# Three places reordered: a second gate bank in the up-projections, the first merge gate scaled inside the attention, a square root ahead of an exponential

## The chip, the core and the metric

The kernel runs on one core of one Trainium2 chip. The metric is the device time in microseconds (us) of one execution of the whole program, taken as the median of several. The engines are TensorE (PE, whose weight loads are shown as PEld), VectorE (DVE), ScalarE (ACT), GpSimd (POOL) and SyncE (SP, which issues the transfers). They run side by side and meet only at semaphores.

## The reference, cut to what matters

Two transformer stacks run one behind the other over 512 tokens of width 1024, all in float32. The first stack has two layers, the second has two. The parts that the change touches:

```python
# first stack, feed forward: causal convolution of width 3 on the gate, exact gelu
u, g = split(h @ w_in, 2)                 # 2816 columns each
g = causal_conv3(g) * w + b
out = (gelu(g) * u) @ w_out
# second stack, per layer
q, k = rope(rmsnorm(q)), rope(rmsnorm(k)) # axial attention: 8 query heads, 2 key heads
p = softmax(q @ k.T); ya = p @ v
z = [y_n @ w_branch[n] for n in range(3)] # ya axial, yb pooling, yc neighbourhood
merged = sum(sigmoid(gl_n + b_n) * z_n for n in range(3))
```

## The kernel before, in words

**Layout.** Activations lie transposed, features in partitions and the 512 tokens in the free dimension, so one tile is 128x512. Every projection is done to about float32 accuracy by splitting both operands in a head and a remainder: one product of 128x128 weights with a 128x512 tile is three matmuls (L476, L477, L478: head by head, head by remainder, remainder by head). A projection over 1024 features is eight such products, 24 matmuls, into one PSUM bank. The eight banks are called PA, PB, S0, S1, T0, T1, O0 and O1. POOL makes the heads and remainders of the weights (L456, L458), in two slots that PE empties in turn; SP refills the raw weights behind it.

**Order of the work.** Each engine has its own program, written out by hand, and the engines wait on counters: `pa_taken` and `pb_taken` say how often the content of PA and PB has been read out, `entry_done` how many weight entries PE has finished, `p_ready` how many exponentials, `pt_copied` how many transposed tiles ACT has copied out. Each engine works strictly in the order of its own program.

**Up-projections (L875 on PE, L1768 on DVE, L1272 on ACT).** There are 22 units, each a gate tile (into PA) and a value tile (into PB). Before unit 0 can be scaled, the norm's factor is needed: PE sums the squares in the middle of the first value tile (L503), ACT takes the root (L1122) and DVE the reciprocal (L1399). DVE then takes the gate (L1777), does the convolution (L1758, L1761, L1761), takes the value (L1782), multiplies it with ACT's gelu (L1788) and writes the remainder (L1790). PE may begin the next gate when PA has been taken, and the next value when PB has. `up` with `squared` false is the first stack's (it runs twice, up0 and up1), with `squared` true the second stack's.

**Axial attention (L662 on PE, L1192 on ACT, L1577 on DVE).** 32 steps t, one per head and query tile, four groups of eight. At an even t PE issues the scores of t and t+1 (L699). DVE scales them and takes their minimum (L1483), ACT takes the exponential (L1169, `soften`), PE transposes it two steps later (L610), ACT copies the transpose out (L1175, `copy_turned`), and PE multiplies by the values three steps later, two heads at once (L742). In between PE fills in parts of the next query projection, three products at t % 8 = 0 and 1, two at 2 in the first three groups; from t = 24 on the slots hold none, one or two products of the next stage. A query group is also normalized on the way: at t % 8 = 5 PE sums squares per head (L815), at t % 8 = 6 ACT takes the root of these sums from bank PB (L1258, `q_root`), at t % 8 = 7 DVE inverts it (L1615). At t = 15, 23, 27 and 35 PE spreads the denominators of a finished group over a bank (L759, `den_turn`): for the first three that bank is PB, and for t = 15 and t = 23 it waits until `q_root` of step 14 or 22 has read PB. ACT copies the spread denominators (L1237), DVE divides (L1525, `y_divide`, at t + 2), ACT and DVE write head and remainder (L1241, L1529, at t + 3 and t + 4). ACT has to load another table when it goes from exponential to root and back (rows named ACT_TABLE_LOAD).

**Merge (L935 on PE, L1280 on ACT, L1793 on DVE).** 24 gates, three per output tile. For each, PE projects the gate into PA (24 matmuls) and the branch into PB (12 matmuls), DVE scales the gate by the norm's factor (L1800), ACT takes the sigmoid (L1287), DVE multiplies it with the branch (L1804 for the first of three, L1806 and L1808 for the others). The first gate and the first branch are projected inside the last twelve steps of the neighbourhood attention, t = 24 to 35; the gate is complete at t = 31. Its scaling by L1800 comes after the whole attention on DVE, so after `y_divide` and the last remainder, and the second gate waits for it since it goes to PA too.

Of the kernel before, what the change touches and what calls it, by code (L numbers as in the profile page):

```python
# [8 lines left out]
ALU = mybir.AluOpType  # L9
# [5 lines left out]
FT = 22  # L15
# [167 lines left out]
def build(nc, x_in, weights, consts, cols_in, lam_in, rel_in, rpb_in, strips_rel, strips_na, out):  # L183
    with ExitStack() as ctx:
# [284 lines left out]
        def _(pe):  # L469
# [192 lines left out]
            def attention(b, b0, kind, last_parts=(), last_plan=()):  # L662
# [18 lines left out]
                def span(t):  # L681
                    return S if full else (t // 2 % 4 + 1) * P
# [20 lines left out]
                for t in range(end + 1):  # L703
                    if t < 32 and t % 2 == 0:
                        score(t); score(t + 1)
                    if t in turns:
                        (y_turn if kind == "diff" else den_turn)(b, turns.index(t), kind)
# [11 lines left out]
                    if 0 <= tt < 32:  # L719
                        if tt < 2:  # L720
                            pe.wait_ge(v_copied, 4 * b["v"] - 1 + tt)
                        pe.wait_ge(p_ready, u + tt + 3)
                        pe.wait_ge(pt_copied, u + tt + 1)
                        transposed(tt, span(tt)).then_inc(pt_ready, 1)
                    tv = t - 3
                    if 0 <= tv < 32:
# [148 lines left out]
            def up(b, squared):  # L875
# [19 lines left out]
                else:  # L895
# [3 lines left out]
                    project(PB[:, :], 1, b["e"] + 1, sum_of=b).then_inc(entry_done, 1)  # L899
                with pe.Fori(1, FT) as i:  # L900
                    gate_and_value(i)
# [149 lines left out]
            H = here  # L1051
# [51 lines left out]
        def _(act):  # L1103
# [88 lines left out]
            def attention(b, kind, ytile, early=None, gain=None):  # L1192
# [4 lines left out]
                for t in range(turns[3] + (2 if kind == "diff" else 4)):  # L1197
                    if t == 4 and early is not None:
                        early()
                    if t < 32:  # L1200
                        soften(u, t, S if full else (t // 2 % 4 + 1) * P,
                               (diff_ready, 4 * b["df"] + max(t // 2 - 1, 0)) if kind == "diff" else None,
                               maps[t // 2 % 2] if kind == "diff" else probs)
# [9 lines left out]
                    if kind == "axial" and t < 24:  # L1213
                        bn = axial_turn(b, t // 8 + 1)
                        if t % 8 == TURN["square"]:
                            q_square(bn["a"] + 2, gain)
                        if t % 8 == TURN["root"]:
                            q_root(bn["r"])
                    if kind == "diff" and t % 2 == 0 and 0 <= t - 8 < 32:
# [154 lines left out]
        def _(dve):  # L1374
# [201 lines left out]

            def attention(b, kind, ytile, after=None):  # L1577

# [9 lines left out]
                for t in range(turns[3] + (3 if kind == "diff" else 5)):  # L1588
# [29 lines left out]
                    if kind != "axial" and t < 24 and t % 8 == K_AT:  # L1618
                        take_k(ahead(g), g + 1)
                    if after is not None and t == 29:  # L1620
                        take_q(after, 0)
# [146 lines left out]
            def up(b, col, two):  # L1768
                per = 5 if two else 2
                taps = [(1, 0), (0, 1), (2, -1)] if two else [(2, 0), (1, 1), (0, 2)]  # L1770
                sum_factor(b)
                with dve.Fori(0, FT) as i:
                    sum_waited(b)
                    chain_at(b["d"] + 1 + i * per)
                    dve.wait_ge(entry_done, b["e"] + 2 * i + 3)
                    dve.wait_ge(gelu_ready, b["z"] + i + 1)
                    TT(GATE[:, :], PA[:, :], rs[:, :], ALU.mult).then_inc(pa_taken, 1)  # L1777
                    dve.wait_ge(pa_taken, b["a"] + i + 2)
# [12 lines left out]
                    done(per)  # L1791

            def merge(b):  # L1793
                with dve.Fori(0, 4) as i:
                    chain_at(b["d"] + i * 2)
                    for q in range(6):
                        n, j = q % 3, 2 * i + q // 3
                        dve.wait_ge(gate_ready, 24 * b["l"] + 6 * i + q + 1)
                        dve.wait_ge(gate_done, 24 * b["l"] + 6 * i + q + 1)
                        TT(tmp[3][:, :], PA[:, :], rs[:, :], ALU.mult).then_inc(pa_taken, 1)  # L1800
                        dve.wait_ge(entry_done, b["e"] + 6 * i + q + 3)
                        dve.wait_ge(gate_done, 24 * b["l"] + 6 * i + q + 2)
                        if n == 0:
                            TT(tmp[1][:, :], PB[:, :], tmp[0][:, :], ALU.mult).then_inc(pb_taken, 1)  # L1804
                        else:
                            TT(tmp[2][:, :], PB[:, :], tmp[0][:, :], ALU.mult).then_inc(pb_taken, 1)  # L1806
                            dve.wait_ge(pb_taken, b["b"] + 6 * i + q + 2)
                            ins = TT(tmp[1][:, :], tmp[1][:, :], tmp[2][:, :], ALU.add)  # L1808
                            if n == 1:
                                link(ins)  # L1810
                            else:
                                ins.then_inc(m_f, 1)

                        if n == 2:
                            dve.wait_ge(m_hi, b["m"] + j + 1)
                            TT(tile(ml, j), tmp[1][:, :], tile(mh, j).bitcast(F), ALU.subtract).then_inc(m_split, 1)
                            dve.wait_ge(m_split, b["m"] + j + 1)
                    done(2)

            def pooling(b, kv, ax, l):  # L1820
# [85 lines left out]
            with dve.Fori(0, LAYERS2) as l:  # L1906
# [3 lines left out]
                v_copy(H("na_v", l))  # L1910
                attention(H("na", l), "na", 8)
                merge(H("merge", l))
# [190 lines left out]
```

## Time and profile before

| what | us |
|---|---|
| median of three runs | 3124.68 (3124.17 to 3125.82) |
| the profiled execution's own time | 3117.95 |
| its span, first to last instruction | 3115.7 |
| PE busy | 3016.9, 97% |
| POOL / DVE / ACT busy | 1659.7 / 1358.7 / 797.9 |
| mean granted TensorE clock | 0.992 of full |

The span is what the hardware profiler saw of the program; the own time is some 2 us more. "Busy" of PE is the time in which a matmul was under way, at whatever clock. The median of the runs is 6.7 us above the profiled execution, 0.2%.

### The profile page before, as it was taken

The page shows a single profiled execution, that of the slowest core. Times are in us where ns is not written, and L with a number is a line of the kernel's source. Part 1 is how long each engine was busy: PE and PEld are TensorE (multiplying, and loading weights), DVE is VectorE, ACT ScalarE, POOL GpSimd, SP SyncE. Part 2 cuts the span into 40 slices and gives each one's busy share as a digit, 9 for nine tenths or more (in the row PEclk, how much of TensorE's full clock was granted, in tenths as well). Part 3 has the DMA queues.
Part 4 walks back from the last instruction along what each step waited for, and adds up shares of the span by engine and source line. Part 5 has one row for each costly group of instructions (what it writes and reads, how often), then busy time and mean ns, then how long its engine had stood idle before and what let it go on. Part 6 is the DMA issues. An engine that isn't in the chain of part 4 may idle for free.

```text
span 3115.7 us, 44683 instructions
## 1 busy us (share of the span) xinstructions
PE 3016.9 (97%) x14804; PEld 2383.8 (77%) x14804; DVE 1358.7 (44%) x2339; ACT 797.9 (26%) x1459; POOL 1659.7 (53%) x1254
## 2 busy tenths in 40 slices
PE   8998999999899999999999999999999999999998
PEld 6766888886578888776678878888767688778886
DVE  3254444223444442243433476640543343576622
ACT  2343221113422220153421122210263411122201
POOL 4334666663156666433346656666324266556674
PEclk9999999999999999999999999999999999999999
DMA  6262223222022233212322222333113222222332
GB/s 160 77 174 73 94 95 107 103 95 74 26 70 92 97 106 107 86 41 67 90 72 91 88 74 97 98 105 104 64 38 90 64 92 97 85 74 96 100 111 78
DMA packets 99746, 276.63 MB, mean 89 GB/s; under 512 B 38014, under 2 KB 38782, under 8 KB 99634
## 3 DMA queue, kind: packets, MB, share of 16 engines
q1 hardware_dynamic: 97184, 269.03, 26.9%
q10 hardware_dynamic: 2450, 6.13, 0.9%
q8 instruction: 67, 1.10, 0.1%
q14 instruction: 45, 0.37, 0.0%
HBM read 271.39 MB, written 11.54 MB: 91 GB/s over the span
## 4 chain that ended last, share of the span: by engine, by line
PE 72%; DVE 2%; issue 1%; ACT 1%; DVEq 0%; ACTq 0%
PE PA L476 11%; PE PA L477 10%; PE PA L478 10%; PE PB L476 9%; PE PB L478 9%; PE PB L477 9%; PE O L742 2%; PE S L699 2%; PE T L610 2%; PE O L508 1%; DVE hl L1409 1%; PE PB L759 0%; DVE tmps L1448 0%; PE O L633 0%; PE S L586 0%
## 5 line engine op out<-in xcount | busy, mean ns | idle before, releaser
L458 POOL TENSOR_TENSOR wl<-raw,wh 128x1024 fp32r<-128x1024 f32 (+2 forms) x416 | 1127.0, 2709 | 33.4
L455 POOL TENSOR_TENSOR zero<-zero 128x1 f32<-128x1 f32 x416 | 82.6, 198 | 1391.4 <-PE PA L478 624.5
L476 PE MATMUL PA<-hh,wh 128*128 128x512 f32 x1328 | 537.1, 404 | 19.4 <-DVE hl L1409 7.1
L477 PE MATMUL PA<-hl,wh 128*128 128x512 f32 x1328 | 521.3, 393 | 0.0
L478 PE MATMUL PA<-hh,wl 128*128 128x512 f32 x1328 | 521.0, 392 | 0.0
L456 POOL CAST wh<-raw 128x1024 fp32r<-128x1024 f32 (+2 forms) x416 | 476.3, 1145 | 0.0
L476 PE MATMUL PB<-hh,wh 128*128 128x512 f32 x896 | 357.8, 399 | 0.0
L478 PE MATMUL PB<-hh,wl 128*128 128x512 f32 x896 | 349.3, 390 | 0.0
L477 PE MATMUL PB<-hl,wh 128*128 128x512 f32 x896 | 349.2, 390 | 0.0
L476 PEld LDWEIGHTS PA<-hh,wh 128*128 128x128 f32 x1328 | 251.9, 190 | 120.1 <-issue 55.5
L478 PEld LDWEIGHTS PA<-hh,wl 128*128 128x128 f32 x1328 | 251.5, 189 | 54.0
L477 PEld LDWEIGHTS PA<-hl,wh 128*128 128x128 f32 x1328 | 252.0, 190 | 51.2 <-issue 2.5
L1169 ACT ACTIVATE probs<-biased,stats 128x512 f32<-128x512 f32 (+2 forms) x224 | 145.2, 648 | 322.7 <-PE T L610 192.4
L1761 DVE SCALAR_TENSOR_TENSOR tmps<-S,cols,tmps 128x511 f32<-128x511 f32 (+1 forms) x264 | 197.9, 750 | 39.6 <-DVE tmps L1761 20.0
L476 PEld LDWEIGHTS PB<-hh,wh 128*128 128x128 f32 x896 | 168.1, 188 | 46.9 <-issue 14.6
L478 PEld LDWEIGHTS PB<-hh,wl 128*128 128x128 f32 x896 | 168.4, 188 | 36.0
L477 PEld LDWEIGHTS PB<-hl,wh 128*128 128x128 f32 x896 | 168.4, 188 | 33.9 <-issue 1.2
L1276 ACT ACTIVATE T<-tmps 128x512 f32<-128x512 f32 x88 | 53.0, 602 | 395.2 <-DVE tmps L1761 395.2
L1278 ACT ACTIVATE acth<-T 128x512 f32 x88 | 52.7, 599 | 333.2 <-DVE T L1788 333.2
L476 PE MATMUL PA<-acth,wh 128*128 128x512 f32 x352 | 137.4, 390 | 0.0
L478 PE MATMUL PA<-acth,wl 128*128 128x512 f32 x352 | 137.0, 389 | 0.0
L477 PE MATMUL PA<-actl,wh 128*128 128x512 f32 x352 | 137.0, 389 | 0.0
(321 smaller groups left out, 4828.3 us busy)
## 6 DMA issues: line engine op xcount, KB each, us to landing
raw<-in_w_up SPq DMA_DIRECT2D x176, 512.0 KB, 3.4
raw<-in_w_down SPq DMA_DIRECT2D x64, 768.0 KB, 4.1
raw<-in_w_merge SPq DMA_DIRECT2D x48, 768.0 KB, 4.2
raw<-in_w_out SPq DMA_DIRECT2D x32, 512.0 KB, 3.4
strips_na<-in_rpb SPq DMA_DIRECT2D x1, 7620.0 KB, 31.5
raw<-in_w_pool SPq DMA_DIRECT2D x12, 512.0 KB, 3.4
raw<-in_w_na_qk SPq DMA_DIRECT2D x12, 512.0 KB, 3.5
raw<-in_w_na_v SPq DMA_DIRECT2D x8, 512.0 KB, 3.4
```

Of the source, the lines that this page charges most:

```text
L455: nc.gpsimd.tensor_tensor(zero[:, :], zero[:, :], zero[:, :], ALU.add)
L456: nc.gpsimd.tensor_copy(wh[s][:, 0:width], raw[s][:, 0:width]).then_inc(w_head, 1)
L458: nc.gpsimd.tensor_tensor(wl[s][:, 0:width], raw[s][:, 0:width], wh[s][:, 0:width].bitcast(F), ALU.subtract).then_inc(w_split, 1)
L476: mm(dst, h_, rh, start=first, stop=False)
L477: mm(dst, h_, rl, start=False, stop=False)
L478: return mm(dst, l_, rh, start=False, stop=last)
L610: last = nc.tensor.transpose(TB[t % 2][:, k * P:k * P + P], src[t % 2][:, k * P:k * P + P], ident[:, :])
L699: mm(SB[head][:, 0:span(t)], queries[g % 2][r, qt * P:qt * P + P], (axial_key if kind == "axial" else keys[g % 2])[r, 0:span(t)], start=Tr ...
L742: last = mm(bank[r, q], values(head, k), probsT[head][:, k * P:k * P + P], start=(k == 0), stop=(k == L // P - 1))
L1169: A(to[t % 2][:, 0:L], biased[t % 2][:, 0:L], ACT.Exp, scale=-1.0, bias=mn[:, t % 8:t % 8 + 1], accum_out=den[:, t % 8:t % 8 + 1]).then_in ...
L1276: A(GELU[:, :], tmp[0][:, :], f).then_inc(gelu_ready, 1)
L1761: ins = STT(out=dst[:, lo:hi], in0=src[:, lo - d:hi - d], scalar=w(k), in1=dst[:, lo:hi], op0=ALU.mult, op1=ALU.add)
```

## The change

Three edits. **(1)** In `up` of the first stack, PE projects the second gate into O0 with no wait on `pa_taken`, and the second value into PB after its own wait; the loop starts at unit 2. DVE does units 0 and 1 ahead of its loop, the second reading its gate from O0. **(2)** DVE scales the merge's first gate at t = 35 of the neighbourhood attention, ahead of `y_divide` of t = 37; the merge's first round on DVE is written out without that step. A wait on `m_split` moves from behind the remainder (L1816) to the next first product of a group. **(3)** In the axial attention ACT does `q_root` at the head of step t, ahead of that step's exponential and copy, and PE does `den_turn` of t = 15 and t = 23 behind the transposition of that step.

```diff
 (PE, attention)
-                    if t in turns:
+                    late = kind == "axial" and t in turns[0:2]
+                    if t in turns and not late:
                         (y_turn if kind == "diff" else den_turn)(b, turns.index(t), kind)
...
                         transposed(tt, span(tt)).then_inc(pt_ready, 1)
+                    if late:
+                        den_turn(b, turns.index(t), kind)
...
 (PE, up)
                     project(PB[:, :], 1, b["e"] + 1, sum_of=b).then_inc(entry_done, 1)
-                with pe.Fori(1, FT) as i:
+                    project(O0[:, :], 0, b["e"] + 2).then_inc(entry_done, 1)
+                    pe.wait_ge(pb_taken, b["b"] + 2)
+                    project(PB[:, :], 1, b["e"] + 3).then_inc(entry_done, 1)
+                with pe.Fori(1 if squared else 2, FT) as i:
                     gate_and_value(i)
...
 (ACT, attention)
+                    if kind == "axial" and t < 24 and t % 8 == TURN["root"]:
+                        q_root(axial_turn(b, t // 8 + 1)["r"])
                     if t < 32:
                         soften(u, t, S if full else (t // 2 % 4 + 1) * P,
...
-                        if t % 8 == TURN["root"]:
-                            q_root(bn["r"])
...
 (DVE, attention)
+                    if gate is not None and t == 35:
+                        take_gate(gate, 0)
...
 (DVE, up)
-                with dve.Fori(0, FT) as i:
+                def unit(i, gate_bank):
...
-                    TT(GATE[:, :], PA[:, :], rs[:, :], ALU.mult).then_inc(pa_taken, 1)
+                    TT(GATE[:, :], gate_bank[:, :], rs[:, :], ALU.mult).then_inc(pa_taken, 1)
...
+                sum_factor(b)
+                if not two:
+                    unit(0, PA)
+                    unit(1, O0)
+                with dve.Fori(0 if two else 2, FT) as i:
+                    unit(i, PA)
...
 (DVE, merge)
+            def take_gate(b, n):
+                dve.wait_ge(gate_ready, 24 * b["l"] + n + 1)
+                dve.wait_ge(gate_done, 24 * b["l"] + n + 1)
+                TT(tmp[3][:, :], PA[:, :], rs[:, :], ALU.mult).then_inc(pa_taken, 1)
...
+                        if q >= taken:
+                            take_gate(b, 6 * i + q)
...
                         if n == 0:
+                            if taken == 0 or q:
+                                dve.wait_ge(m_split, b["m"] + j)
                             TT(tmp[1][:, :], PB[:, :], tmp[0][:, :], ALU.mult).then_inc(pb_taken, 1)
...
-                            dve.wait_ge(m_split, b["m"] + j + 1)
...
+                tiles(0, 1)
+                with dve.Fori(1, 4) as i:
+                    tiles(i, 0)
...
-                attention(H("na", l), "na", 8)
+                attention(H("na", l), "na", 8, gate=H("merge", l))
```

## Rows read from the trace of the kernel before

**Rows 1.** The page, busy us, share of the span and instructions.

```profile
PE 3016.9 (97%) x14804; PEld 2383.8 (77%) x14804; DVE 1358.7 (44%) x2339; ACT 797.9 (26%) x1459; POOL 1659.7 (53%) x1254
```

**Rows 2.** PE's waits: line, waited for, us in total, times, longest us.

```profile
PE PB L759 <- ACT stats L1258: 9.3, 4, 2.3
...
PE PA L476 <- DVE S L1777: 6.2, 2, 3.1
...
PE PA L476 <- DVE tmps L1800: 5.9, 2, 3.0
```

**Rows 3.** PE by stretch: us, busy (matmuls), granted clock, DMA share, GB/s.

```profile
300.00:304.00 4.00, 0.92 (x5) 1.00 0.23 89
...
1419.00:1421.00 2.00, 2.00 (x5) 0.50 0.00 0
1575.00:1578.00 3.00, 2.90 (x7) 0.56 0.00 0
2299.00:2301.00 2.00, 1.87 (x16) 0.50 0.00 0
```

**Rows 4.** Timeline, start of up0: start, us, engine, line [idle before, releaser].

```profile
300.43 0.40 PE L478 MATMUL PB<-hh,wl 128*128 128x512 f32 x1
...
303.90 0.49 PE L476 MATMUL PA<-hh,wh 128*128 128x512 f32 x1 [3.08 <-DVE S L1777]
...
306.78 0.69 DVE L1782 TENSOR_TENSOR tmps<-PB,rs 128x512 f32<-128x512 f32 x1
...
309.86 0.69 DVE L1777 TENSOR_TENSOR S<-PA,rs 128x512 f32<-128x512 f32 x1
...
314.90 0.39 PE L476 MATMUL PA<-hh,wh 128*128 128x512 f32 x1
```

**Rows 5.** Timeline, axial attention of layer 0, steps 13 to 16.

```profile
1388.51 0.58 ACT L1175 ACTIVATE probsT<-T 128x512 f32<-128x512 f32 x1
...
1389.27 1.09 PE L742 MATMUL O<-probsT,tmps 128*64 128x128 f32 x16
...
1391.07 1.28 ACT L1258 ACT_TABLE_LOAD   x1
...
1392.36 0.27 ACT L1258 ACTIVATE stats<-PB,eps 128x8 f32<-128x8 f32 x1
...
1392.68 1.09 PE L759 MATMUL PB<-ident,stats 128*64 128x128 f32 x16 [2.32 <-ACT stats L1258]
...
1395.74 0.72 ACT L1169 ACTIVATE probs<-biased,stats 128x512 f32<-128x512 f32 x1
...
1398.06 1.09 PE L742 MATMUL O<-probsT,tmps 128*64 128x128 f32 x16
```

**Rows 6.** Timeline, the same layer, steps 22 to 24.

```profile
1412.80 0.58 ACT L1175 ACTIVATE probsT<-T 128x512 f32<-128x512 f32 x1
...
1416.97 1.09 PE L759 MATMUL PB<-ident,stats 128*64 128x128 f32 x16 [2.32 <-ACT stats L1258]
...
1423.23 0.99 PE L742 MATMUL O<-probsT,tmps 128*64 128x128 f32 x14
```

**Rows 7.** Timeline, from the neighbourhood attention into the merge, layer 0.

```profile
1565.64 0.17 DVE L1519 RECIPROCAL stats<-stats 128x2 f32<-128x2 f32 x1 [0.28 <-ACT probs L1169]
...
1571.75 0.40 PE L478 MATMUL PB<-yh,wl 128*128 128x512 f32 x1
...
1572.87 0.63 ACT L1241 ACTIVATE yh<-y_tok 128x512 fp32r<-128x512 f32 x1 [0.91 <-DVE y_tok L1525]
1573.90 3.78 POOL L458 TENSOR_TENSOR wl<-raw,wh 128x1536 fp32r<-128x1536 f32 x1
1575.10 0.58 PE L476 MATMUL PA<-hh,wh 128*128 128x512 f32 x1 [2.95 <-DVE tmps L1800]
1577.33 0.69 DVE L1804 TENSOR_TENSOR tmps<-PB,tmps 128x512 f32<-128x512 f32 x1 [2.37 <-ACT tmps L1287]
...
1584.97 0.39 PE L476 MATMUL PA<-hh,wh 128*128 128x512 f32 x1
```

More of the change, by code:

```diff
@@ L1575, in take_k, with attention @@
                 TT(keys[g % 2][:, :], PB[:, :], rs[:, :], ALU.mult).then_inc(pb_taken, 1)
-            def attention(b, kind, ytile, after=None):
+            def attention(b, kind, ytile, after=None, gate=None):
                 u, turns = b["u"], Y_TURN[kind]
@@ L1770, in up @@
                 taps = [(1, 0), (0, 1), (2, -1)] if two else [(2, 0), (1, 1), (0, 2)]
-                sum_factor(b)
-                with dve.Fori(0, FT) as i:
+                def unit(i, gate_bank):
                     sum_waited(b)
@@ L1791, in up, with tiles @@
                     done(per)
+                sum_factor(b)
[8 more added lines that the diff above has]
+                TT(tmp[3][:, :], PA[:, :], rs[:, :], ALU.mult).then_inc(pa_taken, 1)
             def merge(b):
-                with dve.Fori(0, 4) as i:
+                def tiles(i, taken):
                     chain_at(b["d"] + i * 2)
@@ L1797, in merge @@
                         n, j = q % 3, 2 * i + q // 3
-                        dve.wait_ge(gate_ready, 24 * b["l"] + 6 * i + q + 1)
-                        dve.wait_ge(gate_done, 24 * b["l"] + 6 * i + q + 1)
-                        TT(tmp[3][:, :], PA[:, :], rs[:, :], ALU.mult).then_inc(pa_taken, 1)
+                        if q >= taken:
+                            take_gate(b, 6 * i + q)
                         dve.wait_ge(entry_done, b["e"] + 6 * i + q + 3)
```

## The prediction

> **What bounds the kernel now.** I read four views, from the widest to the narrowest. The page shows PE busy for 97% of the span and no other engine above 77% [rows 1]: time is won only where PE waits or runs slowly. PE's waits name three that the change addresses: the denominators' turn waits for ACT's root four times, 9.3 us; the gate of an up-projection waits for DVE's scaling twice, 6.2 us; the merge's second gate waits for DVE's scaling twice, 5.9 us [rows 2]. Together 21.4 us. Two of four turns in each of two layers, two up-projections and two merges make just these eight places, so each is one stall of 2.3 to 3.1 us.
>
> The table by stretch adds what the waits don't hold. After five of the eight stalls PE's granted clock stands at 1.2 instead of 2.4 GHz, for 3 to 4 us each: after both merge stalls, after both turns at t = 23 and after that of t = 15 in layer 1; three of these stand in [rows 3], the other two repeat them. Not after the first stall of layer 0, and not after those of the up-projections, whose row shows the full clock through a wait of 3.1 us [rows 3]. PE is "busy" there, so only the clock shows this loss.
>
> The timelines then tell what is next in line behind each wait, and this decides the gain.
>
> **Part 1, up-projections.** Before: the last matmul of value 0 starts at 300.43 and the pitch of these matmuls is 0.227, so PE could go on at 300.66; it goes on at 303.90, and reaches gate 2 at 314.90 [rows 4]. After: gate 1 goes to O0 at once, 300.66 to 306.11 (24 x 0.227 = 5.45). Then value 1 needs PB, which DVE takes only at 306.78 to 307.47 [rows 4], behind reciprocal, gate and convolution, none of which moves. PE starts some 0.13 us behind such a release (gate 1 did behind the scaling's end), so value 1 starts at 307.60: a new wait of 1.5 us takes the place of half of the old one. Value 1 then needs 5.56 (with the 0.1 that a start after a wait costs), and gate 2 is reached at 313.16 instead of 314.90. Gain 1.7 us, twice: **3.5 us**. Gate 2 in PA waits for both takes; DVE did its second at 309.86 to 310.55 [rows 4], since it was busy with unit 0 until then, so that is met. The weights of entry 2 were ready at the time of the old stall; POOL starts on entry 4 when gate 1 is done (306.1) and needs 3.6 us. The loops begin one unit later on PE; I cost a loop's entry at nothing, since the loop of the second stack's up-projection is entered with no gap above 0.1 us. Were it paid, it would be that.
>
> **Part 2, merge.** DVE's last work of the attention's steps ends at 1565.81 and it then idles until 1572.09, the gate has been complete since step 31, which that last row already lies behind, so the moved scaling (0.69) sits in that idle time and ends by 1566.6 [rows 7]. Its target was last read by the scores of t = 31. PE's last branch matmul starts at 1571.75, so the second gate starts at 1571.98 instead of 1575.10: 3.1 us [rows 7]. It also ran at the lower clock: from 1575.10 to the third gate's start at 1584.97 are 9.87 us for 36 matmuls, which need 8.17 at the full clock: 1.7 us. The second branch, at 1577.4, needs PB taken: ACT's copy ends at 1573.50, table load 1.28 and sigmoid 0.72 follow at once instead of waiting for L1800, so DVE's product, before at 1577.33 [rows 7], comes at 1575.6 to 1576.3. Cover 1.1 us. POOL's split for the third gate ends at 1577.68 [rows 7] and is wanted at 1580.15: cover 2.5 us. Gain 3.12 + 1.70 = 4.8, twice: **9.6 us**. The moved `m_split` wait only lets DVE's next scaling start a trifle earlier, where PE is not waiting: nothing; if DVE lost its slack there it would still be no later than before.
>
> **Part 3, axial turns.** Both halves are needed. In layer 0 PE is free at 1390.30 (the product at 1389.27 [rows 5] and 1.03 of pitch) and stalls until 1392.68. After: the transposition of step 13, whose exponential ACT had done before its copy of 1388.51, goes first, 0.6 us; ACT is free at 1389.09 [rows 5], the sums are long there, so load 1.28 and root 0.27 [rows 5] end at 1390.65. The turn can start at 1390.9 without a wait. Gain 2.4 us here.
>
> What becomes late is the exponential of step 14: it now has a root and a second load before it. ACT's row of work is then: root to 1390.65, load to 1391.95, exponential 14 (0.72) to 1392.7, copy 12 (0.58) to 1393.3, exponential 15 to 1394.0, copy 13 to 1394.6. PE wants exponential 14 at its transposition, behind scores and three products, at 1395.1, and copy 13 at the product that was at 1398.06 [rows 5] and is now due at 1395.68. Cover 1.0 us. The same at steps 22 to 24, where only two products lie between: ACT free at 1413.38 [rows 6], copy 21 at 1413.38 + (1394.6 - 1389.09) = 1418.9; PE's product is due at 1414.6 + 4.7 = 1419.3 (4.7 is the 5.38 us from turn to product in [rows 5] less one product of 0.68). Cover 0.4 us. At step 6, where the root also moves, there is no turn to gain; ACT waits 0.5 us for DVE there, which the root now fills, and the exponentials before step 8's transpositions are met: nothing, at worst 0.5 us each.
>
> The turn at t = 23 of layer 0 took 6.26 us from turn to product [rows 6] against 4.70 at the full clock: 1.56 us, the same in layer 1, and 1.49 at t = 15 of layer 1 (6.87 against 5.38). Gain 4 x 2.4 + 2 x 1.56 + 1.49 = **14.1 us**.
>
> For this ScalarE row the trace has a load of 1.28 us with the next instruction 0.01 us behind it, and the copy ending 0.02 us ahead of it [rows 5]. The Trainium skill ("ScalarE: Activation LUTs", What ACT_TABLE_LOAD costs) speaks against the edit: it counts 1.28 for the load and 1.38 more of drain at every switch, 2.66 in all. By that estimate copy 13 comes 2.8 us later, PE waits 1.8 us at t = 16 and 2.4 at t = 24, and the whole gains 8.4 us less.
>
> **The sum.** 3.5 + 9.6 + 14.1 = 27.2 us, of it 8.0 the clock's. Span 3115.7 to 3088.5; the profiled execution's time 3117.95 to 3090.8; the runs' median stands 6.7 us above that, so 3124.7 to **3097.5**. A measurement of this kernel can tell about 0.2%, 6.2 us, from no change.
>
> **The rivals.**
>
> *A. The waits go, the slow clock stays.* The clock fell after five of eight stalls that look alike, and not after the two longest, so it depends on more than the stall: around it PE does short transpositions and products with gaps. If as many slow stretches fall elsewhere (the norms between stages have such places, some with and some without the fall), 8.0 us are not gained: 3105.5. For it: a clock at half behind stalls of 2.3 us. Against: in the rest of the attention, as thin but without stalls over 1 us, it never fell. The Trainium skill ("TensorE: Matmul & The Clock Gate", What's actually happening) has the clock fall behind idle time of PE; by that rule removed stalls bring the clock back, as I count, and the trace agrees behind five of the eight.
>
> *B. The exponential comes too late.* In [rows 5] the exponential starts 3.11 us behind the root's end (1392.63 to 1395.74), of which I call 1.8 a wait for PE's transposition. Were it the engine's own, copy 13 came at 1396.4 and copy 21 at 1420.8 against 1395.7 and 1419.3: PE waits 0.7 and 1.5 us, in both layers 4.5 us: 3102.0.
>
> *C. Slower.* The exponential late as in B and past all cover, at all six roots and not only at the four with a turn: a wait of 2.3 us at each (two loads and a root, 2.83, less ACT's idle 0.5), each followed by a slow stretch of 1.7, while part 3's own stalls stay: 6 x 4.0 - 13.1 = 10.9 us slower, 3135.6. It decides once exponential 14 ends later than PE arrives, 1395.1 against my 1392.7; against it stands that cover of 2.4 us.
>
> *D. Nothing left of it.* PE's gains are waited back behind POOL or a transfer. PE waits for POOL's weights hardly anywhere and POOL is 53% busy [rows 1], so little speaks for it: 3122 to 3125.
>
> **How the numbers follow.** Forecast 0.70, A 0.14, B 0.09, C 0.03, D 0.04. Likeliest case: 3097.5, itself good to some 4 us (the clock at two or three places either way, 1.7 each). Downwards, if PB's wait in part 1 were absent and one or two slow stretches of the norms vanished with the shift, 7 us more: 3090.5. Upwards the range takes in A and B and some of both, to 3110. Faster by over 0.2%: 0.93; within: 0.04; slower: 0.03.
>
> **What would show it.** PE's waits no longer name the root at L759 nor L1800 at L476; in up0 and up1 the wait for L1777 is gone and one of about 1.5 us for L1782 stands at value 1. The granted clock is 1.00 in the turns and at the start of the merge. In ACT's timeline a root follows a copy at once, and a load and the exponential behind it. Wrong would be: a wait at L610 or L742 for ACT behind the turns (B, C), rows at clock 0.50 in new places (A), new waits for L458 (D).

## The result and the profile after

| | before | after |
|---|---|---|
| median, runs | 3124.43 (3119.70 to 3125.82), 4 runs | 3089.35 (3087.22 to 3091.99), 4 runs |
| ratio, 95% interval | | 0.9894 (0.9882 to 0.9906) |
| the profiled execution's own time | 3117.95 | 3091.99 |
| its span, mean granted clock | 3115.7, 0.992 | 3089.9, 0.995 |

The kernel is 1.1% faster: 35.1 us between the medians, 25.8 us between the two profiled spans. Forecast were 3097.5 us and a gain of 27.2. The median also lies 1.2 us below 3090.5, the lowest case that the prediction worked out. The two gaps differ because before's profiled execution was faster than the four runs beside it, and after's slower than all others of after.

The page of after has 7.1 us less of PE against [rows 1], the work being the same:

```profile
PE 3009.8 (97%) x14804; PEld 2379.3 (77%) x14804; DVE 1355.2 (44%) x2339; ACT 796.2 (26%) x1459; POOL 1655.7 (54%) x1254
```

PE's waits of after (line numbers have moved: L759 is L762, L742 is L745, L1777 is L1784, L1782 is L1789, L1800 is L1810, L1258 is L1264, L1169 is L1175, L1175 is L1181). The three of [rows 2], 21.4 us, are gone. The last row below is the only new name, and it is the wait that the prediction expected at value 1:

```profile
PE O L745 <- ACT probsT L1181: 6.0, 14, 0.9
...
PE PA L476 <- DVE tmps L1704: 3.5, 4, 1.4
...
PE PB L476 <- DVE tmps L1789: 1.2, 2, 0.6
```

PE by stretch, after. The columns are the length in us, the busy time of PE, PEld, DVE, ACT and POOL with their instructions in brackets, the granted clock, the DMA share and GB/s. The rows are the end of step 24 of the axial attention, the start of the merge, and a place in layer 1 that was at full clock before:

```profile
1410.00:1412.00 2.00, 2.00 (x18) 1.57 (x18) 1.29 (x5) 1.32 (x4) 0.00 (x0) 1.00 0.03 8
1560.00:1564.00 4.00, 4.00 (x19) 3.31 (x18) 1.43 (x2) 3.06 (x4) 3.24 (x3) 1.00 0.00 0
2180.00:2183.00 3.00, 3.00 (x13) 2.82 (x13) 2.93 (x6) 1.40 (x4) 0.00 (x0) 0.50 0.00 0
```

So the half clock of [rows 3] is gone behind the turns and in the merge, and a new stretch stands at 2180 to 2187, in the key and value projections of layer 1.

Setting equal pieces of work of the two profiles side by side gives the account, in us (in brackets the sum reached; a minus is a loss):

| from the start to | before | after | gained |
|---|---|---|---|
| up0, gate 2 starts | 314.90 | 312.38 | 2.5 |
| norm behind up1 | 1362.98 | 1357.71 | 2.8 (5.3) |
| axial layer 0, product of t = 24 | 1423.23 | 1411.61 | 6.3 (11.6) |
| merge layer 0, third gate starts | 1584.97 | 1568.61 | 4.7 (16.4) |
| layer 1 before its key projections | 2193.87 | 2177.47 | 0.0 (16.4) |
| behind the new slow stretch | 2269.40 | 2256.28 | -3.3 (13.1) |
| behind the axial turns of layer 1 | 2385.92 | 2364.90 | 7.9 (21.0) |
| behind the merge of layer 1 | 2723.74 | 2697.89 | 4.8 (25.8) |

The parts gained 5.3, 14.2 and 9.6, together 29.1 (forecast: 3.5, 14.1, 9.6), and the new slow stretch took 3.3 back. Of the 5.3 us of part 1, 2.5 belong to each up-projection: from the sum of squares in value 0 (L503) to gate 2 are 17.19 us in before and 14.70 in after, in up0 and up1 alike. The other 0.3 arise near 720 us, far from both, where PE waits 3.61 us for the queries in both kernels and more of a slow stretch lies behind that wait in before.

One half-clock stretch of before costs nothing. In before it stands at 1817.8 behind two short waits for DVE in the norm, and from 1817.80 to 1829.28 PE needs 11.48 us; at full clock, in after, the same work takes 11.49 us (1801.41 to 1812.90), since PE waits for DVE there anyway:

```profile
1818.00:1821.00 3.00, 3.00 (x6) 1.68 (x7) 2.93 (x5) 1.70 (x3) 0.00 (x0) 0.50 0.00 0
1802.00:1805.00 3.00, 2.79 (x9) 1.24 (x7) 2.93 (x6) 1.40 (x4) 0.00 (x0) 1.00 0.00 0
```

The first row is of before, the second of after.

Timeline of after, up0. Buffer numbers are left out, so O is O0. Gate 1 goes to O0 at once, value 1 waits 0.59 us for PB, gate 2 starts at 312.38. Against [rows 4], L1789 starts at 306.06 where L1782 stood at 306.78:

```profile
299.45 3.35 DVE L1405 RECIPROCAL rs<-acc 128x512 f32<-128x512 f32 x1 [6.18 <-ACT acc L1128]
...
300.62 0.39 PE L476 MATMUL O<-hh,wh 128*128 128x512 f32 x1
...
302.84 0.70 DVE L1784 TENSOR_TENSOR S<-PA,rs 128x512 f32<-128x512 f32 x1
...
303.58 0.81 DVE L1766 TENSOR_SCALAR tmps<-S,cols 128x512 f32<-128x512 f32 x1
...
306.06 0.69 DVE L1789 TENSOR_TENSOR tmps<-PB,rs 128x512 f32<-128x512 f32 x1
...
306.81 0.50 PE L476 MATMUL PB<-hh,wh 128*128 128x512 f32 x1 [0.59 <-DVE tmps L1789]
...
312.38 0.39 PE L476 MATMUL PA<-hh,wh 128*128 128x512 f32 x1
```

Timeline of after, axial attention of layer 0, steps 13 to 16, the stretch of [rows 5]. The root follows a load, the load a copy; the turn (L762) has no wait in front of it; the exponential starts right behind its load, and ACT then waits 1.38 us for PE:

```profile
1383.23 0.57 ACT L1181 ACTIVATE probsT<-T 128x512 f32<-128x512 f32 x1
...
1383.83 1.28 ACT L1264 ACT_TABLE_LOAD   x1
...
1385.02 0.66 PE L610 MATMUL T<-ident,probs 128*128 128x128 f32 x4
1385.12 0.27 ACT L1264 ACTIVATE stats<-PB,eps 128x8 f32<-128x8 f32 x1
1385.41 1.28 ACT L1175 ACT_TABLE_LOAD   x1
...
1385.60 1.09 PE L762 MATMUL PB<-ident,stats 128*64 128x128 f32 x16
...
1386.70 0.72 ACT L1175 ACTIVATE probs<-biased,stats 128x512 f32<-128x512 f32 x1
...
1390.57 0.72 ACT L1175 ACTIVATE probs<-biased,stats 128x512 f32<-128x512 f32 x1 [1.38 <-PE T L610]
```

Timeline of after, start of the merge, the stretch of [rows 7]. The gate starts with no wait, and table load, sigmoid and product follow the copy of the branch's operand at once:

```profile
1560.43 0.39 PE L476 MATMUL PA<-hh,wh 128*128 128x512 f32 x1
...
1561.99 1.28 ACT L1293 ACT_TABLE_LOAD   x1
...
1563.28 0.72 ACT L1293 ACTIVATE tmps<-tmps,cols 128x512 f32<-128x512 f32 x1
1564.04 0.69 DVE L1825 TENSOR_TENSOR tmps<-PB,tmps 128x512 f32<-128x512 f32 x1 [1.22 <-ACT tmps L1293]
...
1568.61 0.39 PE L476 MATMUL PA<-hh,wh 128*128 128x512 f32 x1
```

### The profile page after: what moved, and what is told of

It reads as the page before. It is cut to its first block, busy times and chain, and to the rows that moved or that the text cites. A ratio compares the mean times of both kernels' runs of the same rounds, so it can differ in the third digit from the quotient of the medians.

```text
span 3089.9 us, 44657 instructions
## 1 busy us (share of the span) xinstructions
PE 3009.8 (97%) x14804; PEld 2379.3 (77%) x14804; DVE 1355.2 (44%) x2339; ACT 796.2 (26%) x1459; POOL 1655.7 (54%) x1254
## 4 chain that ended last, share of the span: by engine, by line
PE 73%; DVE 2%; issue 1%; ACT 1%; DVEq 0%; ACTq 0%
PE PA L476 11%; PE PA L478 10%; PE PA L477 10%; PE PB L476 9%; PE PB L478 9%; PE PB L477 9%; PE O L745 2%; PE S L699 2%; PE T L610 2%; PE O L508 1%; DVE hl L1415 1%; DVE tmps L1454 0%; PE PB L762 0%; PE O L633 0%; PE S L586 0%
## 5 line engine op out<-in xcount | busy, mean ns | idle before, releaser
L476 PE MATMUL PA<-hh,wh 128*128 128x512 f32 x1312 | 525.8, 401 | 8.9 <-DVE hl L1415 8.9
L478 PE MATMUL PA<-hh,wl 128*128 128x512 f32 x1312 | 512.9, 391 | 0.0
L477 PE MATMUL PA<-hl,wh 128*128 128x512 f32 x1312 | 512.6, 391 | 0.0
L1175 ACT ACTIVATE probs<-biased,stats 128x512 f32<-128x512 f32 (+2 forms) x224 | 145.1, 648 | 318.9 <-PE T L610 191.5
```

Of the source, the lines that this page charges most:

```text
L476: mm(dst, h_, rh, start=first, stop=False)
L477: mm(dst, h_, rl, start=False, stop=False)
L478: return mm(dst, l_, rh, start=False, stop=last)
L1175: A(to[t % 2][:, 0:L], biased[t % 2][:, 0:L], ACT.Exp, scale=-1.0, bias=mn[:, t % 8:t % 8 + 1], accum_out=den[:, t % 8:t % 8 + 1]).then_in ...
```

## The experiments

Three groups: each part alone; each half of part 3 alone; and what set the size of part 1 and of the clock's share. A gain in time is the ratio's distance from 1 times before's median beside it. The diffs are cut to what matters. Before ran 15 times beside each of the three sets of runs, with medians of 3121.82 (e1 to e3), 3122.18 (e4 to e7) and 3120.15 us (e8 to e11).

### Each part alone

**e1_up**: before with the up-projections' edit only (PE's side is shown; DVE's is that of the change).

```diff
+                    project(O0[:, :], 0, b["e"] + 2).then_inc(entry_done, 1)
+                    pe.wait_ge(pb_taken, b["b"] + 2)
+                    project(PB[:, :], 1, b["e"] + 3).then_inc(entry_done, 1)
-                with pe.Fori(1, FT) as i:
+                with pe.Fori(1 if squared else 2, FT) as i:
```

> Only part 1, the second gate in O0. Theory (parts add, each gain sits at its own place): the same as in the changed kernel's trace, gate 2 of up0 2.5 us earlier than before, the one of up1 another 2.8, and a wait of 0.6 us for DVE at value 1 in place of one of 3.1 at gate 1; time 5.3 us below the kernel before, ratio 0.998. My prediction had 3.5 us and a wait of 1.5. Rival (only the predicted 3.5 belongs to the edit and the rest to what the other parts shift): gate 2 is 1.7 us earlier in each, ratio 0.999. The stalls of the axial turns (2.3 us, four) and of the merge (3.0 us, two) stay as before; where the clock falls behind them may differ, 1.6 us each.

Measured: 3113.99 us (11 runs), ratio 0.9976 (0.9967 to 0.9985), 7.5 us with an interval of 4.7 to 10.3. PE waits 0.59 us at value 1 of each, and from L503 to gate 2 are 14.70 and 14.71 us, as in after. So the whole 2.5 us a place belong to this edit, and the rival's 1.7 falls. The other two parts' waits stand as before (9.3 and 5.9 us).

**e2_merge**: before with the merge's edit only (the line that moves the scaling is shown).

```diff
+                    if gate is not None and t == 35:
+                        take_gate(gate, 0)
```

> Only part 2, the merge's first gate scaled ahead of the last division, with the moved wait on m_split. Theory: PE's second gate starts right behind the last branch matmul in both layers, at a clock of 1.00, the third gate is reached 4.8 us earlier per layer, 9.6 us in all, ratio 0.997. Rival (the clock falls there for the thin attention in front of it and not for the stall): the second gate still runs at 0.50 to 0.60 for some 3 us and only 3.1 us per layer are gained, 6.2 us, ratio 0.998.

Measured: 3109.01 us (5 runs), ratio 0.9964 (0.9951 to 0.9978), 11 us. The merge's wait is gone, the other two stand. From the second gate to the third are 8.17 us in both layers, against 9.87 and 9.89 in before: the clock stays whole, and the rival falls.

**e3_axial**: before with both halves of the axial edit only.

```diff
+                    if late:
+                        den_turn(b, turns.index(t), kind)
 (ACT)
+                    if kind == "axial" and t < 24 and t % 8 == TURN["root"]:
+                        q_root(axial_turn(b, t // 8 + 1)["r"])
```

> Only part 3, the root ahead of the exponential and the denominators' turn behind the transposition. Theory: four stalls of 2.3 us go and the clock stays at 1.00 through steps 14 to 26, the products at L742 of steps 16 and 24 are 2.4 to 4.0 us earlier, 14 us in all, ratio 0.9955. Rival A (the clock falls all the same): 9.5 us, ratio 0.997. Rival B (the exponential of step 14 or 22 is late): waits of 0.7 to 1.5 us for ACT at the product of steps 16 and 24, and 4.5 us less.

Measured: 3106.34 us (5 runs), ratio 0.9957 (0.9943 to 0.9970), 13.4 us. No wait for the root is left, and no slow stretch in steps 14 to 26.

What follows: each part gains by itself. The gains rank as forecast, but their intervals overlap (4.7 to 10.3, 6.9 to 15.3 and 9.4 to 17.8 us), so the times do not prove the order. Their sum, 32 us, fits the 33 of the whole by its ratio, and each part's waits go without touching the others'; the times alone could not tell an interplay of a few us.

### Which half of the axial edit

**e4_root_only**: before, ACT's root moved, the turn left where it was.

> Half of part 3: ACT takes the root ahead of the exponential, PE keeps the turn in front of the transposition. Theory (the root's early end does nearly all, since it ends 0.4 us behind PE's arrival): the stall at the turn shrinks from 2.3 to 0.3 to 0.4 us, the clock stays up, and the kernel is within 2 us of part 3 alone: 12 to 13 us below before, ratio 0.996. Rival (both halves are needed, as I predicted): the turn in front of the transposition delays the exponential of step 15 too, and the gain is under 8 us, ratio 0.9975 or more.

**e5_late_only**: before, the turn behind the transposition, the root left where it was.

> The other half of part 3: PE does the turn of t = 15 and 23 behind the transposition, ACT keeps the root behind exponential and copy. Theory: the root ends at the same time as before, so PE does 0.6 us of transposition in the old stall and then waits 1.7 us; 0.6 us gained four times, 2.4 us, and the slow clock behind the stalls where it was, ratio 0.999. Rival: the earlier transposition lets ACT go straight from root to exponential 15 (1.8 us earlier on ACT) and PE picks up more than 1 us each, and the shorter stall keeps the clock: 8 us, ratio 0.9975.

**e11_no_late**: after, with the turn put back ahead of the transposition.

```diff
-                    late = kind == "axial" and t in turns[0:2]
-                    if t in turns and not late:
+                    if t in turns:
...
-                    if late:
-                        den_turn(b, turns.index(t), kind)
```

> After, with the denominators' turn put back ahead of the transposition (the root stays ahead of the exponential). By what the root alone did to before (a wait of 0.36 us left at each of the four turns), the kernel waits four times 0.36 us more than after: 1.4 us, 3091 us, with no half-speed stretch behind the turns. Rival, the prediction's (both halves are needed): a wait of 1.0 us or more at each turn, and 3094 us or above.

Measured: e4 3111.62 us (5 runs), ratio 0.9964 (0.9951 to 0.9978), 11 us; e5 3114.90 us (11 runs), 0.9979 (0.9970 to 0.9988), 6.6 us; e11 3093.48 us (5 runs), beside 3094.43 us of after on the same chip (e9). PE's waits for the root in e4:

```profile
PE PB L759 <- ACT stats L1258: 1.4, 4, 0.4
```

In e5:

```profile
PE PB L762 <- ACT stats L1261: 6.9, 4, 1.7
```

And in e11:

```profile
PE PB L759 <- ACT stats L1261: 1.4, 4, 0.4
```

The root's move alone cuts the stall from 2.32 to 0.36 us, and the moved turn alone to 1.73. With the root moved, the turn's half is worth 4 x 0.36 = 1.4 us by the waits, which the times of e11 and e9 can't tell from nothing. The time of e11 lies between its two expectations, 3091 and 3094 us or more; its wait of 0.36 us against the rival's 1.0 decides. "Both halves are needed" was wrong.

In e5 the waits fell by only 9.3 - 6.9 = 2.4 us and the time by 6.6. None of its four stalls of 1.73 us is followed by the half clock. So the expectation had the waits right and the clock wrong, and its rival the reverse. PE by stretch, e5, two of the four turns at which [rows 3] or its kind had 0.50:

```profile
1422.00:1424.00 2.00, 2.00 (x21) 1.07 (x18) 0.01 (x1) 1.99 (x4) 0.00 (x0) 1.00 0.00 0
...
2302.00:2304.00 2.00, 2.00 (x19) 1.07 (x16) 0.18 (x1) 1.99 (x4) 0.00 (x0) 1.00 0.03 8
```

### What sets the size of part 1

**e6_loops**: after, DVE's units 0 and 1 each in a loop of one trip.

```diff
-                    unit(0, PA)
-                    unit(1, O0)
+                    with dve.Fori(0, 1) as i:
+                        unit(i, PA)
+                    with dve.Fori(1, 2) as i:
+                        unit(i, O0)
```

> The changed kernel with DVE's units 0 and 1 of the first stack's up-projections each in a loop of one trip, so that their addresses come from registers as in the kernel before; PE's program is that of the changed kernel. Theory (the 1.8 us that part 1 gained beyond the prediction come from DVE's straight code, whose instructions follow each other by 0.03 us and not by 0.15 to 0.30): DVE's gaps are back, it takes value 0 some 3.7 us behind the gate's start as before, PE waits 1.4 us at value 1, and gate 2 of up0 starts 0.8 to 0.9 us later than in the changed kernel, that of up1 the same: 1.7 us slower than the changed kernel. Rival (the gaps come from the waits, not from the registers): no difference in DVE's gaps, same time as the changed kernel.

Measured: 3093.21 us (5 runs), ratio 0.9908 (0.9894 to 0.9921); value 1 waits 0.58 us as in after, and DVE's operations follow each other by 0.03 to 0.10 us. The expectation missed: a loop of one trip does not bring the gaps back. The reason lies in the trace's records of DVE's register steps, which the views leave out. In before six such steps of 0.04 to 0.12 us stand in the gaps between the reciprocal and the taking of the value: two ahead of the gate's scaling, two ahead of the convolution's first operation and one ahead of each of its other two. In e6 there is none, as in after. So this loop did not restore what it was meant to restore, and the run only shows that a loop around the unit does not by itself cause the gaps.

**e10_peel**: before, DVE's units 0 and 1 written out ahead of the loop, banks and PE's order as before.

```diff
+                if not two:
+                    unit(0)
+                    unit(1)
-                with dve.Fori(0, FT) as i:
+                with dve.Fori(0 if two else 2, FT) as i:
+                    unit(i)
```

> Before, with units 0 and 1 of VectorE's first-phase up loop written out ahead of the loop, and nothing else (banks and TensorE's order stay). Theory: what separates VectorE's operations by 0.15 to 0.30 us in the loop is the register work between them; written out, they follow each other by 0.03. So the scaling of gate 1 starts 0.2 us earlier behind the reciprocal, the stall of 3.08 us is 2.88, unit 0's last operation starts some 0.9 us earlier, and everything behind the stall comes 0.2 us earlier at each of the two places: 0.4 us in all, too little for the time to show (3120 to 3122 us, same). Rival: the spacing comes from the data's path (the banks, the semaphores) and stays at 0.15 to 0.30, the stall at 3.08. That part 1 gained 2.5 us a place and not 1.7 would then be the bank's doing alone.

Measured: 3122.08 us (11 runs), ratio 1.0003 (0.9994 to 1.0012), the same. DVE's timeline of e10, up0:

```profile
301.77 3.35 DVE L1399 RECIPROCAL rs<-acc 128x512 f32<-128x512 f32 x1 [6.18 <-ACT acc L1122]
305.16 0.70 DVE L1777 TENSOR_TENSOR S<-PA,rs 128x512 f32<-128x512 f32 x1
305.90 0.81 DVE L1758 TENSOR_SCALAR tmps<-S,cols 128x512 f32<-128x512 f32 x1
...
308.38 0.69 DVE L1782 TENSOR_TENSOR tmps<-PB,rs 128x512 f32<-128x512 f32 x1
```

and PE's wait there:

```profile
PE PA L476 <- DVE S L1777: 5.8, 2, 2.9
```

From the reciprocal's start to that of L1782 are 308.38 - 301.77 = 6.61 us, as in after (306.06 - 299.45 = 6.61); in before they were 7.29 (306.78 in [rows 4], the reciprocal at 299.49). So writing the unit out, with no bank changed, takes 0.68 us off DVE's row of work, and 0.2 off the first stall (3.1 to 2.9). The six register steps of before are absent in e10 too. The rival, that the gaps come from the banks and the semaphores, falls.

**e7_value_bank**: after, value 1 into S1 instead of PB.

```diff
-                    pe.wait_ge(pb_taken, b["b"] + 2)
-                    project(PB[:, :], 1, b["e"] + 3).then_inc(entry_done, 1)
+                    project(S1[:, :], 1, b["e"] + 3).then_inc(entry_done, 1)
```

> The changed kernel with the second value in the free bank S1, so that PE waits for nothing at it. Theory (the wait of 0.6 us at value 1 is all that is left in part 1, and DVE is done with gate 1 in O0 before PE wants PA for gate 2): the wait at value 1 is gone, gate 2 of up0 and up1 0.7 us earlier, 1.4 us below the changed kernel. Rival (the wait only moves on to gate 2, since DVE takes gate 1 at 308.9 to 309.6 in the changed kernel and PE would be there at 311.5): no wait by these numbers; if DVE's take came later than 311.5 the gain would be smaller by what it is late.

Measured: 3089.67 us (4 runs), ratio 0.9897 (0.9882 to 0.9913). PE's waits for L1789 are gone. Its timeline, value 1 and gate 2:

```profile
309.96 0.39 PE L476 MATMUL S<-hh,wh 128*128 128x512 f32 x1
...
315.40 0.39 PE L476 MATMUL PA<-hh,wh 128*128 128x512 f32 x1
```

Gate 1 started at 304.52 in this execution, so it is 10.88 us to gate 2 against 312.38 - 300.62 = 11.76 in after: 0.9 us less at each of two places, 1.8 us. It is the fastest version by its profile (span 3087.8), but runs of after on two chips differ by more (3089.35 and 3094.43, below), so its time proves nothing against after's.

### Where the half clock falls

**e8_before_again** and **e9_after_again**: the two kernels unchanged, profiled a second time.

> The kernel before, unchanged, profiled a second time. If the half-speed stretches of TensorE follow from the kernel's stalls alone (theory F), the same stretches stand at the same places as in the first profile: behind the axial turn of step 24 and the merge's first entry of layer 0, behind the axial turn of step 16 of layer 1. If a stall of 2 to 3 us only opens a chance of one, which falls anew in each execution (theory G), the stretches stand behind a partly other set of the same ten stalls, some also at places without a stall, and the span differs from 3115.7 us by 1.5 to 3 us for each more or less: I expect G, and a span of 3113 to 3123 us. The stalls themselves (3.08, 2.32 and 2.95 us) have the same lengths in both theories.

> The kernel after, unchanged, profiled a second time and timed in more runs beside the kernel before. The stretch at half speed at 2178 to 2188 us, which took back 3.3 us in the first profile, is a matter of that execution (theory G): it is gone or stands elsewhere. If it is a new wait or a new pattern that the change brought (rival), it is there again. The median lies at 3089.5 us, within 1.5, and the ratio to before at 0.989 to 0.991 in both. Places reached, against the first profile, agree within 0.1 us wherever neither has a slow stretch behind it.

Measured: e8 3121.92 us, span 3120.1; e9 3094.43 us (5 runs), ratio 0.9913 (0.9899 to 0.9926), span 3090.6. After's median in e9 lies 3.4 us above the upper end expected, and the ratio just leaves the range given. The waits have the lengths of the first profiles. PE by stretch, e8:

```profile
307.00:309.00 2.00, 2.00 (x5) 1.61 (x6) 1.58 (x3) 0.00 (x0) 0.55 (x1) 0.50 0.23 25
1397.00:1399.00 2.00, 1.90 (x22) 1.56 (x24) 0.20 (x1) 0.18 (x2) 0.00 (x0) 1.00 0.00 0
1423.00:1425.00 2.00, 2.00 (x6) 0.51 (x4) 0.00 (x0) 1.57 (x2) 0.00 (x0) 0.50 0.00 0
```

Behind the first up-projection's stall, where [rows 3] had 1.00, the clock is now at half; behind the first turn it is whole in both. The five stalls that had the half clock behind them in the first profile have it again, so e8 has six of eight. PE by stretch, e9. The first row is the work that ran at 0.50 from 2180 on in after's first profile, the second a place ahead of everything that the change touches:

```profile
2182.00:2188.00 6.00, 6.00 (x43) 5.25 (x43) 5.90 (x10) 3.60 (x7) 0.00 (x0) 1.00 0.00 0
258.00:262.00 4.00, 4.00 (x11) 3.12 (x10) 1.67 (x2) 1.56 (x3) 2.43 (x2) 0.50 0.51 133
```

The new stretch is gone, and one that the first profile of after did not have stands at 256 to 263, behind a wait of 3.30 us for ACT that all kernels have. e9 trails the first profile by 4.04 us at 1803.41 against 1799.37, and by only 0.70 at 2698.59 against 2697.89: 3.3 us are back. Of the 4.04, 3.51 stand already at value 1 of up0 (310.32 against 306.81), most of them behind the stretch at 256 to 263. The other 0.5 arise at 719 to 723, where e9 still runs at half clock and the first profile does not:

```profile
719.00:723.00 4.00, 4.00 (x11) 3.11 (x10) 0.00 (x0) 1.44 (x5) 0.00 (x0) 0.50 0.72 205
719.00:723.00 4.00, 4.00 (x20) 2.77 (x19) 0.86 (x7) 0.00 (x0) 0.00 (x0) 1.00 0.24 65
```

The first row is e9, the second after's first profile. So one kernel's stretches differ from execution to execution, at places that recur. The stretch of layer 1 stood once more, in e11 at 2180 to 2187. Of the five profiles with all parts, or all but the moved turn, two had it (after and e11, not e6, e7 and e9), and of the eight others none; that is too few to say whether the change made it more likely.

With eight stalls an execution, the profiles of all kernels that still have them give a count. It pools kernels with differing edits. A stall counts as followed where a window of 2 us right behind it has a clock under 0.97; the shorter stalls are from e1, e4, e5, e6, e9, e11 and after.

| stall | us | followed by the half clock |
|---|---|---|
| merge's second gate | 2.95 | 14 of 14 |
| up's second gate | 2.9 to 3.1 | 6 of 14 |
| axial turn | 2.32 | 10 of 20 |
| axial turn in e5 | 1.73 | 0 of 4 |
| value 1, or turn in e4 and e11 | 0.35 to 0.59 | 0 of 18 |

The same count at four waits that the change leaves alone, in all 13 profiles, keeps the length of a stall from being the whole answer:

| wait | us | followed by the half clock |
|---|---|---|
| queries, near 715 | 3.6 | 13 of 13 |
| ACT, near 256 | 3.3 | 9 of 13 |
| two waits in a norm, 2 us apart, near 1816 and 2724 | 1.16 and 1.08 | 13 of 26 |
| key projections of layer 1, near 2178 | 1.23 | 2 of 13 (after, 2.2 us behind it, and e11) |

What a followed stall costs can be read from one piece of work in all profiles. From the merge's second gate to its third the stretch costs 1.5 to 1.8 us in eleven cases, but 2.8 to 3.0 in three (layer 0 of e1, e4 and e10: 11.17, 11.06 and 10.98 us against 8.17), where it is twice as long. Behind the turns and the up-projections' stalls it costs 1.4 to 1.6.

## Why the prediction was right, and where it was not

**What bounds the kernel** was right: the 21.4 us of [rows 2] were all on PE's path, and no wait of the same size took their place.

**Part 1 was mis-sized.** The step that failed: the take of PB at 306.78 to 307.47, "behind reciprocal, gate and convolution, none of which moves". The order did not move, but DVE's pace did: written out, its operations follow each other by 0.03 to 0.10 us instead of 0.10 to 0.30. The take ended at 306.75, value 1 waited 0.59 us instead of 1.5, and gate 2 came at 312.38 instead of 313.16. e10 shows 0.68 us of this with nothing else changed. The gain was 2.5 us at each place, 5.0 for 3.5. What differs in DVE's records between before and e10 are the register steps in the gaps; no run took them away alone, so that they are the whole cause is the likeliest reading and not shown.

**Part 2 was right** in each term: the second gate starts right behind the branch, the clock is whole, and product and split come in time: 4.7 and 4.8 us for 4.8 each. Its clock term, 1.7 twice, was the safest of the prediction: that stall was followed by the half clock in 14 cases of 14. That both of before's stretches there were short ones was luck, by the three long ones among the 14.

**Part 3 was right in its sum (14.2 for 14.1) and wrong in one step.** The sum holds for before's first profile, in which three of the four turns had the half clock behind them (4.6 us of the 14.1); by the count, one in two, some 3.1 us are to be expected, which one profile could not tell. "Both halves are needed" failed: e4 shows 0.36 us left of 2.32 with the root alone, and e11 the same from the other side. The prediction saw that ACT is free at 1389.09 and a load and a root take 1.56 us; that ends at 1390.65 against PE's 1390.30, so a wait of 0.35 us with the root alone could be worked out from its own numbers. The moved turn only puts the transposition into these 0.35 us.

**Rivals B and C** (the exponential too late) fell: in [rows 5] the exponential came 3.11 us behind the root's end, and in after it comes 1386.70 - 1385.39 = 1.31 behind, its load being all that lies between. The difference of 1.8 us was indeed a wait for PE's transposition. The Trainium skill ("ScalarE: Activation LUTs", What ACT_TABLE_LOAD costs) counts a drain of 1.38 us more at each switch. This case's trace does not agree: the root starts 0.01 us behind its load's end, and the next load 0.02 us behind the root's. The 8.4 us which that rule took off the gain were not lost.

**Rival A** (the slow stretches fall elsewhere) came true in part and in one execution: 3.3 us at 2180 in the first profile of after, none in the second. So it does not follow from the change alone. By the counts above an execution of before has 2 + 2 x 6/14 + 4 x 10/20 = 4.9 such stretches behind its stalls; at 1.7 us each they are 8.3 us (8.2 with the measured cost of each kind), where the prediction counted 8.0 from one profile. With 5.0 us net of waits in part 1, 5.9 in part 2 and 9.3 in part 3 that makes 28.5 us. The four measurements lie around it: 25.8 and 29.5 us between profiled spans (first and second pair), 35.1 and 25.7 between medians.

**The final step, from the profile to the median, failed.** The prediction kept the 6.7 us by which before's median stood above its profiled execution. They belonged to no kernel: before's profile was faster than the runs beside it, after's median lies 2.6 us below its profile. 8.1 us separate 3097.5 from 3089.35; 1.5 are part 1's. The rest is most likely the same chance of slow stretches in a few executions: in before's 45 later runs the time follows the clock (median 3116.3 us at a mean clock of 0.993 in 3 runs, 3121.9 at 0.991 in 26, 3124.0 at 0.989 in 6), and after's runs on the first chip had 0.995 or 0.996, on e9's 0.993 or 0.994. Why one set draws fewer stretches stays open. The 3090.5 that the prediction named as its lowest case was passed for another reason than it gave: the wait for PB did not vanish, and the half-clock stretches of the norms, both absent in after's first profile, cost nothing.

## What to carry to other kernels

Price a stall together with the clock behind it, and count that clock from several executions: one profile shows which stretches fell, not which can. When an edit writes loop trips out, measure the engine's pace in straight code elsewhere in the trace before keeping the loop's spacing in a sum. Before calling two edits inseparable, subtract what each leaves; here one was worth nearly all.

## What the hardware showed

- The half clock behind a stall differs between executions of one kernel. At the places of the change 30 of 48 stalls of 2.3 to 3.1 us were followed by it, and none of 22 shorter ones of 0.35 to 1.73. Length alone does not decide: 2.95 us in the merge gave it always, 3.08 us in the up-projections 5 times in 12, and two waits of 1.16 and 1.08 us close together 13 times in 26. What decides no run shows.
- What a half-clock stretch costs depends on the place: 1.4 to 1.8 us for most behind the stalls, nothing in the norm at 1817.8, where PE waits for DVE.
- A table load on ACT took 1.28 us with gaps of 0.01 to 0.03 us on either side, also twice in a row around a root of 0.27.
- A unit of seven DVE operations in the loop lost 0.68 us up to its fifth operation against the same unit written out. Its gaps hold register steps of 0.04 to 0.12 us each, which the unit written out does not have.
